# GpSimd's low-part subtractions of 1024 columns made in four instructions of 256 columns each

## The chip, the cores and the metric

The kernel runs on 1 core of one Trainium2 chip. The metric is the device time of one execution in microseconds (us): the median of 3 runs of the kernel before is 2904.75 us (2903.07 to 2905.82). Five engines work beside each other and meet only in semaphores: TensorE (PE; its weight loads are PEld), VectorE (DVE), ScalarE (ACT), GpSimd (POOL) and SyncE (SP, which only issues DMAs here).

## The reference, cut to what matters

A chain of two models over 512 tokens of width 1024: a first layer (compressed, selected and windowed attention, retention, a gated feed-forward network, FFN, with a causal depthwise convolution of width 3), and then a block of two layers (pooling, convolution and differential attention, a squared-ReLU network, a gated embedding). What matters for the change is the one shape in which nearly all of it is computed, a product of a weight with the activations:

```
proj = h @ w_in[layer]
u = causal_dwconv(h @ w_ffn_up[layer], ffn_conv_w[layer], ffn_conv_b[layer])
u_gate, u_val = jnp.split(u, 2, axis=-1)
x = x + (jax.nn.silu(u_gate) * u_val) @ w_ffn_down[layer]
```

Everything is in float32. The kernel makes a float32 product out of three fp32r products: each operand x is split into a high part, x rounded to fp32r, and a low part, x minus its high part, and w*a is w_hi*a_hi + w_hi*a_lo + w_lo*a_hi.

## The kernel before, in words

All weights are one stream, cut into units of 128 partitions by 1024 columns (`UNIT`); two units are a block, four a group. Each unit goes through four steps, on four engines:

1. SP loads a block into `raw` (two slots). Before it overwrites a slot it waits until the low parts of both units of the slot are made (`lo_done`, L294 to L295).
2. ACT copies a unit from `raw` to `w_hi`, which rounds it (`hi_part`, L385), once PE is done with the unit that had the place (`unit_done`): the part of unit u can be made when PE has finished unit u-4.
3. POOL subtracts, `w_lo = raw - w_hi` (`lo_part`, L316), once ACT's `hi_done` has risen, and raises `lo_done` by 1. It does this for 447 profiled units, in order.
4. PE waits for `lo_done` and for the PSUM bank (`evac`), and makes the unit's 24 matmuls with 512 moving columns, L635 to L637 (`unit` and `product`). DVE then reads the PSUM bank (L1059 and others) and does what the layer wants.

Each engine works in the order of its own program; POOL also does a small part of retention (L331 to L347, on 512 and 1024 columns) and seven additions of 512 columns in each layer of the second block (L361).

Around it DVE splits activations in the same way. In the FFN one tile of the hidden width takes two units of PE (gate, then value), and on DVE the sequence L1059, L1468, L1471, L1475 for the gate (into `tile_c`), the same four for the value (into `td`), and then L1484 (product), L1489 (`y_hi`) and L1491 (`y_lo`). L1059 reads one operand from PSUM; the others have all of theirs in SBUF. ACT's Silu of `tile_c` stands in ACT's order between the high parts of two pairs of units, so POOL gets its units in pairs there. The 22 tiles are made in three chunks of 8, 8 and 6; behind each chunk come 8 units of the down projection, which read all `y` tiles of the chunk and wait for each of them in turn.

In retention and in the layers' attention DVE makes the probabilities between two products of PE (L1255 to L1266; L1609 to L1614), and PE waits for the last of them.

At the end of a product that ends a layer part, DVE adds each unit to `h` (L1447), makes the next operand (L1077, L1080) and the sum of squares (L1086, L1090), and PE sums over partitions (L668).

Of the kernel before, what the change touches and what calls it, by code (L numbers as in the profile page):

```python
# [25 lines left out]
ALU = mybir.AluOpType  # L26
# [9 lines left out]
EPS = 1e-6  # L36
UNIT = 8 * P
BLOCK = 2 * UNIT


HEADS, KVG, DH = 8, 2, 64
# [21 lines left out]
U_CMP = NSA_UNITS  # L63
# [13 lines left out]
GROUPS = UNITS // 4  # L77
# [63 lines left out]
def build(nc, stream, xT, tab, decay, rope, par1, par2, pT, out):  # L141
    ctx = ExitStack()
    with ctx:
        def sb(name, shape, dt=F32):
            return ctx.enter_context(nc.sbuf_tensor(name, shape, dt))

        def sem(name):
            return ctx.enter_context(nc.semaphore(name))
# [10 lines left out]

        raw = sb("raw", [P, 2, BLOCK])  # L160
        w_hi = sb("w_hi", [P, 2, BLOCK], F32R)
        w_lo = sb("w_lo", [P, 2, BLOCK], F32R)

# [62 lines left out]
        lo_done = sem("unit_lo_done")  # L226
# [52 lines left out]
        def conv_unit_slot(j):  # L279
            return (j // 2) % 2, slice((j % 2) * UNIT, (j % 2 + 1) * UNIT)  # L280


        @block.sync
        def _(sp):

            sp.dma_start(par[:, 0:C1_FFN], par1[:, 0:C1_FFN]).then_inc(first_gain_landed, 16)
            for k in range(KD):
                sp.dma_start(h[:, k, :], xT[:, k, :]).then_inc(x_tile_landed[k], 16)
            sp.dma_start(raw[:, 0, UNIT:], stream[0, :, UNIT:]).then_inc(landed[0], 16)
            sp.dma_start(raw[:, 1], stream[1]).then_inc(landed[1], 16)  # L290
            with sp.Fori(1, GROUPS) as g:
                for s in range(2):

                    sp.wait_ge(lo_done, g * 4 - 2 + 2 * s)  # L294
                    sp.dma_start(raw[:, s], stream[g * 2 + s]).then_inc(landed[s], 16)  # L295

            for s in range(2):
                sp.wait_ge(lo_done, GROUPS * 4 - 2 + 2 * s)
                sp.dma_start(raw[:, s], stream[s]).then_inc(landed[s], 16)
            for s in range(2):  # L300
                sp.wait_ge(landed[s], 16 * (GROUPS + 1))

            for n in range(KD):
                sp.wait_ge(h_tile_ready, KD * LAYERS + n + 1)
                sp.dma_start(out[:, n, :], h[:, n, :]).then_inc(out_stored, 16)
            sp.wait_ge(out_stored, 16 * KD)


        @block.gpsimd
        def _(pool):  # L310
            def lo_part(u, j):

                s, cols = conv_unit_slot(j)

                pool.wait_ge(hi_done, u + 1)
                pool.tensor_tensor(w_lo[:, s, cols], raw[:, s, cols], w_hi[:, s, cols],  # L316
                                   ALU.subtract).then_inc(lo_done, 1)

            with pool.Fori(0, U_RET // 4) as g:
                for j in range(4):  # L320
                    lo_part(g * 4 + j, j)
            for j in range(3):
                lo_part(U_RET + j, j)

            with pool.Fori(0, RH) as t:
                for j in range(3, RET_UNITS + 3):
                    lo_part(t * RET_UNITS + U_RET + j, j % 4)

                pool.wait_ge(activated, t + 2)
                pool.wait_ge(squares_ready, t + 1)  # L330
                pool.tensor_tensor(rg[:, 0, :], rg[:, 0, :], rq, ALU.mult).then_inc(output_gated, 1)  # L331
                pool.tensor_tensor(rg[:, 1, :], rg[:, 1, :], rk, ALU.mult).then_inc(output_gated, 1)
                pool.wait_ge(output_gated, t * 2 + 2)

                pool.tensor_tensor(rg, rg, small[:, 24:26].unsqueeze(2).to_broadcast([P, 2, S]), ALU.mult)\
                    .then_inc(output_scaled, 1)
                pool.wait_ge(output_scaled, t * 3 + 1)

                pool.wait_ge(root_inverted, t + 1)
                for e in range(2):  # L340
                    pool.tensor_tensor(rg[:, e, :], rg[:, e, :], tile_c, ALU.mult)\
                        .then_inc(output_scaled, 1)
                pool.wait_ge(output_scaled, t * 3 + 3)
                hi, lo = (y[:, bass.ds(t * 2, 2), :] for y in (y_hi, y_lo))
                pool.tensor_copy(hi, rg).then_inc(output_rounded, 1)
                pool.wait_ge(output_rounded, t + 1)
                pool.tensor_tensor(lo, rg, hi, ALU.subtract).then_inc(y_tile_ready, 2)  # L347
            lo_part(U_YA + 3, 3)
            with pool.Fori(U_YA // 4 + 1, U_L // 4) as g:
                for j in range(4):  # L350
                    lo_part(g * 4 + j, j)
            with pool.Fori(0, LAYERS) as layer:
                ul = layer * L_UNITS + U_L
                for j in range(3):
                    lo_part(ul + j, j)

                for k in range(1, KD):
                    pool.wait_ge(x_square_ready, layer * KD + (KD + k + 1))
                    if k > 1:
                        pool.wait_ge(squares_added, layer * (KD - 2) + (k - 1))  # L360
                    ins = pool.tensor_tensor(ssum[:, :], m[:, 0, :] if k == 1 else ssum[:, :], m[:, k, :], ALU.add)  # L361
                    if k < KD - 1:
                        ins.then_inc(squares_added, 1)
                ins.then_inc(squares_ready, 1)
                lo_part(ul + 3, 3)
                with pool.Fori(1, L_UNITS // 4) as g:
                    for j in range(4):
                        lo_part(ul + g * 4 + j, j)
            for j in range(3):
                lo_part(GROUPS * 4 + j, j)  # L370
# [246 lines left out]
        def _(pe):  # L617
# [10 lines left out]
            def product(dst, w, rhs_hi, rhs_lo, nk, first=None, start=True, stop=True):  # L628

                s, c0 = w  # L630
                for k in range(nk):
                    if first is not None:
                        first(k)
                    cols = slice(c0 + k * P, c0 + (k + 1) * P)
                    pe.matmul(dst, w_hi[:, s, cols], rhs_hi(k), start=start and k == 0, stop=False)  # L635
                    pe.matmul(dst, w_hi[:, s, cols], rhs_lo(k), start=False, stop=False)  # L636
                    ins = pe.matmul(dst, w_lo[:, s, cols], rhs_hi(k), start=False,  # L637
                                    stop=stop and k == nk - 1)
                return ins

            def unit(u0, j, lag, dsts, rhs, nk, first=None, start=True, stop=True):


                s, cols = conv_unit_slot(j)
                pe.wait_ge(lo_done, u0 + (j + 1))
                pe.wait_ge(evac, u0 + (j + 5 - lag))
                hi, lo = rhs
                for o, dst in enumerate(dsts):
                    ins = product(dst, (s, cols.start + o * nk * P), hi, lo, nk,
                                  first if o == 0 else None, start, stop)  # L650
                ins.then_inc(unit_done, 1)
# [28 lines left out]
            def simple(u0, j, banks=2, first=None, nk=8):  # L680
                unit(u0, j, banks, [bank[j % banks][:, :]], a_op(), nk, first)
# [34 lines left out]
            def hidden_unit(kv, q):  # L716
                j = kv * 4 + q
                s, cols = conv_unit_slot(j)
                pe.wait_ge(lo_done, U_CMP + j + 1)
                if q == 0:  # L720

                    pe.wait_ge(evac, U_CMP + 3 + kv)
                dst = bank[kv][0:KVG * NCMP, 0:CMP_HIDDEN]
                for k in range(4):
                    w = slice(cols.start + k * CMP_HIDDEN, cols.start + (k + 1) * CMP_HIDDEN)
                    x_hi, x_lo = (x[kv][:, 4 * q + k].rearrange("p g c -> p (g c)") for x in (xc_hi, xc_lo))
                    pe.matmul(dst, x_hi, w_hi[:, s, w], start=q == 0 and k == 0, stop=False)
                    pe.matmul(dst, x_lo, w_hi[:, s, w], start=False, stop=False)
                    ins = pe.matmul(dst, x_hi, w_lo[:, s, w], start=False, stop=q == 3 and k == 3)
                ins.then_inc(unit_done, 1)  # L730
# [37 lines left out]
            with repeat(pe, RH, [(score, 8), (prb, 8), (ptp, 8), (ptr, 8), (pv, 8), (ofree, 1),  # L768
                                 (rin, 4), (rps, 9), (rfree, 8), (sums, 1), (sump, 1),
                                 (tin, 1)]) as t:  # L770
                u0 = t * RET_UNITS + U_RET
# [139 lines left out]
            with repeat(pe, LAYERS, [(a_rdy, 24), (y_rdy, 54), (sums, 15), (sump, 15), (tin, 4),  # L911
# [43 lines left out]
                for j in range(8):  # L955
                    if j == 7:
# [4 lines left out]
                         lambda k, j=j: square_sum((b_r0, b_r1)[(j - 1) % 2], ones2, (tile_b, tile_c)[(j - 1) % 2])  # L961
# [915 lines left out]
def _stream(x):  # L1877
# [54 lines left out]
    both = np.stack(units).reshape(UNITS // 2, 2, P, UNIT)  # L1932
    return np.ascontiguousarray(both.transpose(0, 2, 1, 3)).reshape(UNITS // 2, P, BLOCK)

# [57 lines left out]
```

## Time and profile before

| what | us |
| --- | --- |
| median of 3 runs | 2904.75 (2903.07 to 2905.82) |
| span of the profiled execution | 2901.3 |
| PE busy | 2688.2 (93%) |
| DVE busy | 1791.4 (62%) |
| POOL busy | 1162.9 (40%) |
| ACT busy | 798.3 (28%) |

The profile is of one execution: its span is from its first to its last instruction, and the runs' median is 3.4 us above it. Start and idle times in the views are in us from the start of the span. "Idle" is the time before an instruction in which its engine did nothing, and the name behind the arrow ended it. A DVE or POOL instruction counts as busy from the moment it is taken up, also while it stands still: a group whose minimum and maximum lie far apart on one shape has such standing time in it.

### The profile page before, as it was taken

The numbers are of one execution on the slowest core, as the hardware profiler recorded it, in microseconds if no ns is written. First come the engines' busy times: TensorE is split into PE (matmuls) and PEld (weight loads), VectorE is DVE, ScalarE is ACT, GpSimd is POOL, SyncE is SP. The second block draws the span as 40 slices with busy tenths as digits, with TensorE's granted clock in tenths as the row PEclk, the third lists the DMA queues.
The fourth block names the chain that finished last, engine by engine and source line by source line (L and its number), as shares of the span: only waits on it lengthen the run. The fifth ranks groups of instructions, "written<-read, shape, count | busy, mean of one in ns | idle before, by whom it ended". The sixth has DMA issues, their size and how long they took to land.

```text
span 2901.3 us, 33803 instructions
## 1 busy us (share of the span) xinstructions
PE 2688.2 (93%) x11835; PEld 2135.0 (74%) x11835; DVE 1791.4 (62%) x2170; ACT 798.3 (28%) x1178; POOL 1162.9 (40%) x493
## 2 busy tenths in 40 slices
PE   7898889999797978989999999999988999999998
PEld 5676666878586866667887788877766887788886
DVE  7566675368666586885238555473888136844484
ACT  2332333313221123433322121124333232211212
POOL 3523332543343444223444444445323444444444
PEclk9999999999898988999999999999999999999999
DMA  4301111322222221112222222222211222222222
GB/s 166 117 33 58 41 39 40 128 88 86 73 87 81 93 87 68 56 62 91 93 96 93 97 97 91 101 102 73 80 58 66 102 92 97 88 102 87 101 101 102
DMA packets 36822, 247.25 MB, mean 85 GB/s; under 512 B 4464, under 2 KB 4848, under 8 KB 7792
## 3 DMA queue, kind: packets, MB, share of 16 engines
q1 hardware_dynamic: 34704, 238.57, 23.2%
q10 hardware_dynamic: 2016, 7.35, 0.7%
q8 instruction: 61, 1.00, 0.1%
q14 instruction: 41, 0.34, 0.0%
HBM read 243.81 MB, written 2.10 MB: 85 GB/s over the span
## 4 chain that ended last, share of the span: by engine, by line
PE 62%; DVE 28%; issue 6%; ACT 1%; POOL 1%; DVEq 1%; ACTq 0%; POOLq 0%
PE bank L635 10%; PE bank L636 10%; PE bank L637 10%; PE both L635 9%; PE both L636 9%; PE both L637 9%; DVE td L1471 2%; DVE td L1475 1%; POOL w_lo L316 1%; DVE y_hi L1063 1%; DVE y_lo L1065 1%; ACT prob L466 1%; DVE small L1218 1%; DVE prob L1266 1%; PE bank L668 1%
## 5 line engine op out<-in xcount | busy, mean ns | idle before, releaser
L316 POOL TENSOR_TENSOR w_lo<-raw,w_hi 128x1024 fp32r<-128x1024 f32 x447 | 1102.0, 2469 | 1633.1 <-ACT w_hi L385 1627.1
L385 ACT ACTIVATE w_hi<-raw 128x1024 fp32r<-128x1024 f32 x446 | 468.4, 1056 | 1032.3 <-PE both L637 532.4
L635 PE MATMUL bank<-a_hi,w_hi 128*128 128x512 f32 x1369 | 564.5, 412 | 3.9 <-POOL w_lo L316 3.2
L637 PE MATMUL bank<-a_hi,w_lo 128*128 128x512 f32 x1369 | 538.8, 394 | 0.0
L636 PE MATMUL bank<-a_lo,w_hi 128*128 128x512 f32 x1369 | 538.2, 393 | 0.0
L635 PE MATMUL both<-a_hi,w_hi 128*128 128x512 f32 x864 | 348.8, 404 | 31.7 <-DVE a_lo L1526 18.9
L637 PE MATMUL both<-a_hi,w_lo 128*128 128x512 f32 x864 | 339.3, 393 | 0.0
L636 PE MATMUL both<-a_lo,w_hi 128*128 128x512 f32 x864 | 339.2, 393 | 0.0
L635 PEld LDWEIGHTS bank<-a_hi,w_hi 128*128 128x128 f32 x1369 | 261.1, 191 | 68.4 <-issue 12.4
L636 PEld LDWEIGHTS bank<-a_lo,w_hi 128*128 128x128 f32 x1369 | 261.1, 191 | 57.9 <-issue 7.3
L637 PEld LDWEIGHTS bank<-a_hi,w_lo 128*128 128x128 f32 x1369 | 259.9, 190 | 56.4
L635 PE MATMUL both<-y_hi,w_hi 128*128 128x512 f32 (+1 forms) x600 | 242.1, 403 | 62.0 <-DVE y_lo L1491 48.2
L636 PE MATMUL both<-y_lo,w_hi 128*128 128x512 f32 (+1 forms) x600 | 238.8, 398 | 0.0
L637 PE MATMUL both<-y_hi,w_lo 128*128 128x512 f32 (+1 forms) x600 | 238.1, 397 | 0.0
L635 PE MATMUL bank<-y_hi,w_hi 128*128 128x512 f32 (+1 forms) x600 | 235.9, 393 | 0.0
L636 PE MATMUL bank<-y_lo,w_hi 128*128 128x512 f32 (+1 forms) x600 | 234.2, 390 | 0.0
L637 PE MATMUL bank<-y_hi,w_lo 128*128 128x512 f32 (+1 forms) x600 | 234.0, 390 | 0.0
L635 PEld LDWEIGHTS both<-a_hi,w_hi 128*128 128x128 f32 x864 | 164.2, 190 | 74.1 <-DVE a_lo L1526 21.4
L636 PEld LDWEIGHTS both<-a_lo,w_hi 128*128 128x128 f32 x864 | 164.3, 190 | 37.9 <-issue 4.5
L637 PEld LDWEIGHTS both<-a_hi,w_lo 128*128 128x128 f32 x864 | 164.0, 190 | 34.7
L635 PEld LDWEIGHTS both<-y_hi,w_hi 128*128 128x128 f32 x600 | 115.5, 193 | 97.3 <-DVE y_lo L1491 51.6
L1063 DVE CAST y_hi<-ta 128x512 fp32r<-128x512 f32 x72 | 147.2, 2044 | 2.5
(272 smaller groups left out, 3270.1 us busy)
## 6 DMA issues: line engine op xcount, KB each, us to landing
raw<-stream SPq DMA_DIRECT2D x223, 1024.0 KB, 4.7
h<-xT SPq DMA_DIRECT2D x8, 256.0 KB, 6.3
h<-xT ACTq DMA_DIRECT2D x1, 2048.0 KB, 7.5
outT<-h SPq DMA_DIRECT2D x8, 256.0 KB, 2.4
h<-decay ACTq DMA_DIRECT2D x1, 1024.0 KB, 4.8
h<-rope ACTq DMA_DIRECT2D x1, 1024.0 KB, 7.0
prob<-pT ACTq DMA_DIRECT2D x2, 512.0 KB, 3.6
par<-par ACTq DMA_DIRECT2D x2, 408.0 KB, 3.1
```

The lines of the kernel that those rows point to most:

```text
L316: pool.tensor_tensor(w_lo[:, s, cols], raw[:, s, cols], w_hi[:, s, cols], ALU.subtract).then_inc(lo_done, 1)
L385: act.activation(w_hi[:, s, cols], raw[:, s, cols], ACT.Copy).then_inc(hi_done, 1)
L466: ins = act.activation(dst, src, ACT.Exp, bias=small[:, b:b + 1], scale=last_scale, accum_out=small[:, b + 4:b + 5])
L635: pe.matmul(dst, w_hi[:, s, cols], rhs_hi(k), start=start and k == 0, stop=False)
L636: pe.matmul(dst, w_hi[:, s, cols], rhs_lo(k), start=False, stop=False)
L637: ins = pe.matmul(dst, w_lo[:, s, cols], rhs_hi(k), start=False, stop=stop and k == nk - 1)
L668: pe.matmul((b_r1 if dst is None else dst)[:, :], ones if w is None else w, ssum[:, :] if src is None else src, start=True, stop=True)\
L1063: V.tensor_copy(y_hi[:, at, :], src).then_inc(vector_step, steps.up())
L1065: V.tensor_tensor(y_lo[:, at, :], src, y_hi[:, at, :], ALU.subtract)\
L1218: V.tensor_reduce(small[:, 8 + cmp:10 + cmp], scores[:, :, 0:n], AX.X, ALU.max)\
L1266: V.tensor_scalar(prob[:, 1, 0:n], prob[:, 1, 0:n], small[:, 14:15], gate[2], ALU.mult, ALU.mult).then_inc(probs_ready, prb.up())
L1471: V.scalar_tensor_tensor(out=dst, in0=buf[:, 15:15 + S], scalar=cw[1], in1=dst, op0=ALU.mult, op1=ALU.add)\
```

## The change

Each subtraction of 1024 columns in `lo_part` becomes four of 256 columns, one behind the other, each of which raises `lo_done` by 1; so `lo_done` counts quarters, and all waits for it (SP's before a load, PE's before a unit and before a unit of the compression) are multiplied by four. No engine waits for a single quarter: PE and SP go on when the fourth is done.

```
+LO_PARTS = 4
@@ sync
-                    sp.wait_ge(lo_done, g * 4 - 2 + 2 * s)
+                    sp.wait_ge(lo_done, g * (4 * LO_PARTS) + (2 * s - 2) * LO_PARTS)
-                sp.wait_ge(lo_done, GROUPS * 4 - 2 + 2 * s)
+                sp.wait_ge(lo_done, (GROUPS * 4 - 2 + 2 * s) * LO_PARTS)
@@ gpsimd, lo_part
-                pool.tensor_tensor(w_lo[:, s, cols], raw[:, s, cols], w_hi[:, s, cols],
-                                   ALU.subtract).then_inc(lo_done, 1)
+                for q in range(LO_PARTS):
+                    part = slice(cols.start + q * UNIT // LO_PARTS, cols.start + (q + 1) * UNIT // LO_PARTS)
+                    pool.tensor_tensor(w_lo[:, s, part], raw[:, s, part], w_hi[:, s, part],
+                                       ALU.subtract).then_inc(lo_done, 1)
@@ tensor, unit
-                pe.wait_ge(lo_done, u0 + (j + 1))
+                pe.wait_ge(lo_done, u0 * LO_PARTS + (j + 1) * LO_PARTS)
@@ tensor, hidden_unit
-                pe.wait_ge(lo_done, U_CMP + j + 1)
+                pe.wait_ge(lo_done, (U_CMP + j + 1) * LO_PARTS)
```

POOL's program in the loop that covers the rest of the first layer (the one over groups at L349 of the kernel before), one group of four units, before:

```order
L316 TENSOR_TENSOR w_lo<-raw,w_hi 128x1024 [waits unit_hi_done]
L315 REGISTER_ALU
L316 TENSOR_TENSOR w_lo<-raw,w_hi 128x1024 [waits unit_hi_done]
L315 REGISTER_ALU
L316 TENSOR_TENSOR w_lo<-raw,w_hi 128x1024 [waits unit_hi_done]
```

The same place of POOL after the change; the lines have moved down by three:

```order
L319 TENSOR_TENSOR w_lo<-raw,w_hi 128x256 [waits unit_hi_done]
L319 TENSOR_TENSOR w_lo<-raw,w_hi 128x256 x3
L316 REGISTER_ALU
L319 TENSOR_TENSOR w_lo<-raw,w_hi 128x256 [waits unit_hi_done]
L319 TENSOR_TENSOR w_lo<-raw,w_hi 128x256 x3
```

The order of the units is as before; the first quarter carries the wait for ACT, and the other three follow it without one. PE's program at the head of a loop over FFN tiles, the first unit of an iteration, before:

```order
L131 UNCONDITIONAL_BRANCH
L131 ISA
L635 MATMUL both<-a_hi,w_hi 128x512 [waits unit_evacuated,unit_lo_done]
L636 MATMUL both<-a_lo,w_hi 128x512
L637 MATMUL both<-a_hi,w_lo 128x512
```

And after the change:

```order
L132 UNCONDITIONAL_BRANCH
L132 ISA
L649 REGISTER_ALU [waits unit_lo_done]
L638 MATMUL both<-a_hi,w_hi 128x512 [waits unit_evacuated]
L639 MATMUL both<-a_lo,w_hi 128x512
L640 MATMUL both<-a_hi,w_lo 128x512
```

In the loops PE has one more register instruction ahead of most units, which works out the multiplied value and takes over the wait for the low part; no matmul has moved. In the retention loop such an instruction stood there before as well, and a second is added to it.

## Rows read from the trace of the kernel before

**Rows 1.** The page, part 1 (its first figures), and part 5, POOL's largest group.

```profile
PE 2688.2 (93%) x11835; PEld 2135.0 (74%) x11835; DVE 1791.4 (62%) x2170; ACT 798.3 (28%) x1178; POOL 1162.9 (40%) x493
...
L316 POOL TENSOR_TENSOR w_lo<-raw,w_hi 128x1024 fp32r<-128x1024 f32 x447 | 1102.0, 2469 | 1633.1 <-ACT w_hi L385 1627.1
```

**Rows 2.** Waits of PE, whole span: us in total, times, longest us.

```profile
PE both L635 <- DVE y_lo L1491: 48.2, 6, 9.5
PE both L808 <- DVE prob L1266: 34.4, 13, 8.2
...
PE bank L941 <- DVE prob L1614: 21.2, 16, 2.7
...
PE bank L668 <- DVE ssum L1090: 14.3, 3, 5.6
PE both L635 <- DVE y_lo L1065: 11.0, 9, 2.2
...
PE bank L635 <- POOL w_lo L316: 3.2, 2, 2.4
```

**Rows 3.** Forms of L1471, L1059, L1526: ns min/median/max, first and last start.

```profile
L1471 DVE SCALAR_TENSOR_TENSOR td<-tb,par,td x22: 751/2926/2948, 676.8 to 1047.8; 128x512 f32<-128x512 f32 x22
...
L1059 DVE TENSOR_TENSOR ta<-bank,rstd x57: 690/692/694, 70.8 to 2890.6; 128x512 f32<-128x512 f32 x57
...
L1526 DVE SCALAR_TENSOR_TENSOR a_lo<-h,mix_gain,a_hi x16: 745/747/1781, 1100.4 to 2005.4; 128x512 fp32r<-128x512 f32 x16
```

**Rows 4.** Timeline of DVE, two FFN tiles: start us, us, instruction.

```profile
703.32 2.94 DVE L1471 SCALAR_TENSOR_TENSOR td<-tb,par,td 128x512 f32<-128x512 f32 x1
706.41 2.65 DVE L1475 SCALAR_TENSOR_TENSOR td<-tb,par,td 128x512 f32<-128x512 f32 x1
...
718.15 2.66 DVE L1484 TENSOR_TENSOR td<-td,tile_c 128x512 f32<-128x512 f32 x1
720.96 2.40 DVE L1489 CAST y_hi<-td 128x512 f32 x1
...
729.79 2.92 DVE L1471 SCALAR_TENSOR_TENSOR td<-tb,par,td 128x512 f32<-128x512 f32 x1
```

**Rows 5.** Timeline of POOL, the first of the same two tiles.

```profile
703.32 5.19 POOL L316 TENSOR_TENSOR w_lo<-raw,w_hi 128x1024 fp32r<-128x1024 f32 x2 [6.74 <-ACT w_hi L385]
```

**Rows 6.** Timelines: POOL's 512-column products in retention; DVE beside POOL's additions L361.

```profile
202.23 1.26 POOL L331 TENSOR_TENSOR work<-work,h 128x512 f32<-128x512 f32 x1 [4.36 <-DVE ssum L1389]
203.45 1.28 POOL L332 TENSOR_TENSOR work<-work,h 128x512 f32<-128x512 f32 x1
...
1101.77 8.19 DVE L1526 SCALAR_TENSOR_TENSOR a_lo<-h,mix_gain,a_hi 128x512 fp32r<-128x512 f32 x6
```

**Rows 7.** Stretches: us, busy us (instructions) of each engine, PEclk, DMA share, GB/s.

```profile
670.00:1090.00 420.00, 363.07 (x1541) 294.70 (x1539) 288.35 (x281) 89.77 (x97) 168.13 (x68) 0.93 0.24 85
...
1580.00:1900.00 320.00, 318.11 (x1397) 261.49 (x1396) 177.28 (x167) 63.11 (x60) 144.45 (x59) 1.00 0.27 95
```

**Rows 8.** Timeline of PE where the first chunk's down projection begins.

```profile
764.15 0.80 PE L635 MATMUL both<-y_hi,w_hi 128*128 128x512 f32 x1 [5.97 <-DVE y_lo L1491]
...
775.25 0.80 PE L635 MATMUL both<-y_hi,w_hi 128*128 128x512 f32 x1 [9.45 <-DVE y_lo L1491]
```

**Rows 9.** Timelines of POOL and DVE, a retention head's second group.

```profile
228.51 7.05 POOL L316 TENSOR_TENSOR w_lo<-raw,w_hi 128x1024 fp32r<-128x1024 f32 x3
...
231.00 2.31 DVE L1264 TENSOR_SCALAR work<-work,small 128x31 f32<-128x31 f32 x1
```

**Rows 10.** Timelines of DVE and PE, end of a layer's squared-ReLU network.

```profile
1931.79 2.26 DVE L1077 TENSOR_SCALAR a_hi<-h,par 128x512 fp32r<-128x512 f32 x1
1934.08 2.90 DVE L1080 SCALAR_TENSOR_TENSOR a_lo<-h,par,a_hi 128x512 fp32r<-128x512 f32 x1
...
1938.49 2.07 PE L668 MATMUL bank<-ssum,cst 128*128 128x512 f32 x2 [5.56 <-DVE ssum L1090]
```

**Rows 11.** Timeline of POOL in the compression.

```profile
107.40 7.15 POOL L316 TENSOR_TENSOR w_lo<-raw,w_hi 128x1024 fp32r<-128x1024 f32 x3 [0.42 <-ACT w_hi L385]
```

**Rows 12.** Forms of L646 and L645 on PE's queue: ns min/median/max, first and last start.

```profile
L646 PEldq ALU_OP  x128: 32/32/42, 115.0 to 2859.2; - x128
...
L645 PEldq ALU_OP  x222: 32/32/36, 122.0 to 2886.4; - x111
```

## The prediction, made before the changed kernel was run

> **What bounds the kernel now.** I read the page's shares first: PE is busy for 2688.2 of 2901.3 us [rows 1], so at most 213 us can be won without taking a matmul away, and the question is who holds PE up in those. The waits of PE answer it: nearly all of the long ones end with a DVE instruction (48.2 us on `y_lo` of the FFN, 34.4 us on retention's probabilities, 21.2, 14.3 and 11.0 us on three others), and next to nothing with POOL (3.2 us) [rows 2]. POOL itself waits 1627.1 us for ACT [rows 1]. So a faster or slower POOL matters little for its own sake, and DVE's speed at a few places matters.
>
> Then I asked of those DVE instructions whether they take as long as they must. They don't: L1471 on `td` is one shape, with a minimum of 751 ns and a median of 2926 [rows 3]. The timelines show what it stands for. At 703.32 POOL and L1471 begin together; L1471 takes 2.94 us instead of 0.75, and ends at 706.26, while POOL's pair of units runs to 708.51. L1475 begins at 706.41 and takes 2.65 instead of 0.75 [rows 4, 5]. So a DVE instruction on SBUF data stands still while one POOL unit runs, gets in between two units, and the next one stands for the second unit. L1484 and L1489 show the same at 718.15 and 720.96 [rows 4]. L1059, with one operand in PSUM, never does: 690 to 694 ns over 57 instances [rows 3].
>
> The Trainium skill's SBUF page (SBUF — State Buffer, section "Who interferes with whom") says the same of this pair: a DVE instruction with two SBUF inputs, or in a two-port mode, and a GpSimd instruction that reads SBUF exclude each other, and whoever comes first keeps the port for its whole instruction. By that rule the length of the POOL instruction is what a DVE instruction pays, and the rows above agree (2.19 and 1.90 us).
>
> **What a 256-column piece costs DVE.** I need the time by which the piece outlasts the DVE instruction ahead of it, since POOL gets its turn there. For 1024 columns: L1475 stands 2.65 - 0.75 = 1.90 us and had begun 0.15 us after the end of L1471, so 2.05 us [rows 4]. For 512 columns: L1526 stands 1.781 - 0.745 = 1.04 us beside L361 [rows 3]; in the stretch of six, two free and four held ones add up to 8.61 us in 8.19, so each begins 0.08 us before the one ahead has ended, which gives 0.96 us [rows 3, 6]. A line through both has 2.13 ns a column and gives 0.41 us for 256. A DVE instruction behind the usual gap of 0.15 us then stands some 0.27 us, one that begins early 0.49 us, and one that starts together with the first piece 2.19 - 768 x 2.13 ns = 0.55 us. Bounds: nothing, where the piece runs beside L1059 or while DVE is idle; 1.04 us, if a short instruction held DVE as long as the 512-column one. I take the line, which has two measured points, and keep both ends.
>
> **The FFN, step by step.** Two tiles take 26.47 us (703.32 to 729.79), 13.24 a tile, of which 2.19 + 1.90 + 1.97 + 1.97 over two tiles is standing time [rows 4]: 4.0 a tile, 9.2 without. PE needs two units of 24 matmuls: 318.11 / 1397 = 0.228 us a matmul at full clock [rows 7], 10.9 us. So DVE falls behind by 2.3 us a tile, 18 to 19 over a chunk of eight, and PE waits for it when the down projection wants the last `y` tiles: 5.97 and 9.45 us in the first chunk [rows 8], 48.2 in six waits for the three chunks [rows 2]. After the change a tile has eight pieces. Starting with L1484: 0.5, then 0.27 and 0.29; L1059 (0.69 us and its gaps, off the port) lets two pieces by almost free, 0.1; the last three cost 0.27, 0.27 and nothing beside the other L1059. Sum 1.7. Starting with L1471 it is 2.0. A tile is then 10.9 to 11.2 us, DVE holds PE's pace within 0.3 us, and what is left is the latency of the last tile: some 5 us of DVE work behind the last value unit with 1 to 2 us of pieces, against 7/8 of a unit (4.8 us) that PE can do meanwhile, plus a small backlog. I put what PE still waits at 3 us a chunk: 48 - 9 = **-39 us**. PE also works at the lower clock there (granted 0.93 [rows 7]): 1541 matmuls at 363.07/1541 - 0.228 = 0.008 us are 12 us, of which I give back 5: **-5**.
>
> **Retention.** Three units of POOL in a row (7.05 us) meet L1261, L1264 and L1266, which stand 2.1 us each (L1264: 2.31 us for an instruction on 31 columns) [rows 9]; PE waits up to 8.2 us for L1266, 34.4 in 13 waits [rows 2]. With pieces each stands at most 0.49 us: 6.2 becomes 1.5, -4.7, three times; in some five other waits one unit holds L1266, 1.3 us each. 14 + 6 = 20, of which I take **-18**, since DVE's remaining pieces fall on its next instructions.
>
> **Other ends.** L1077 and L1080 stand 1.77 and 2.15 us behind the last unit of a layer part, and DVE was already behind from the units ahead; PE waits 5.56 us [rows 10], 14.3 in all [rows 2]. I take -10. Of the 11.0 and 21.2 us on L1065 and L1614 [rows 2] I take -6 and -5, about 1 us where a held instruction stands last, and -2 at the start of the program. Together **-23**.
>
> **What it costs.** POOL: 512 columns take 1.26 us and follow each other after 1.22 [rows 6], 1024 take 7.15 / 3 = 2.38 [rows 11]. By the line a piece takes 0.64 to 0.70 and four 2.6 to 2.8: +0.2 to +0.4 a unit. POOL's 1627.1 us of waiting for ACT [rows 1] cover that nearly everywhere. They don't in the compression, where PE takes a unit as fast as POOL makes it: 8 units x 0.3 = **+2.5**. Beside DVE a pair of units stretches from 5.19 us to eight turns of about 1.0, and POOL has 6.74 us free ahead of the pair now [rows 5]; that is just enough at 11 us a tile. SP's loads start by as much later; a slot has the time of two units. Stretched units also meet DVE instructions that were free before; for all of that **+5**.
>
> The GPSIMD Engine Reference of the Trainium skill ("Performance versus the Vector engine", section 3.1) speaks against the change: it measures 4497 ns for a two-input instruction of 2048 elements. Beside the 2.38 us for 1024 here, an estimate from that page is 0.26 us fixed for each instruction, +0.8 us a unit and +6 instead of +2.5 in the compression; no run of before has 256 columns.
>
> PE: one more register instruction ahead of each unit in the loops. PE has such ones now, of 32 ns (128 that also wait for `lo_done`, 222 that don't) [rows 12], and through the loop of 1580 to 1900 with them its matmuls follow at 0.228 us without idle time [rows 7]: nothing. If they were exposed it would be 447 x 0.032 = +14 us, which I keep for the upper end.
>
> **Sum.** -39 - 5 - 18 - 23 + 2.5 + 5 = -77.5 on a span of 2901.3, so 2824 for the span, and with the 3.4 us by which the median lies above it, 2827 us.
>
> **The rivals.**
> - *The standing time is only spread.* POOL needs the port just as long; if each of the four pieces meets a DVE instruction that has begun early, it is 4 x 0.49 = 1.96 us, what one unit costs now. For it: DVE is dense there, busy 288 of 420 us [rows 7]. Against it: the gaps of 0.15 us and L1059 in each tile. A tile is then 13.24 - 4.0 + 2.6 = 11.8 us, the backlog 7 us a chunk; the FFN gives 22 instead of 44, the rest about half of 41, the costs stay: -35, about 2870 us.
> - *DVE does not get in between pieces.* No engine waits between them, and the GPSIMD page (section 2.1) says that a GpSimd core begins its next instruction as soon as its own share is done. If the port then stayed with POOL over all four, DVE would stand as now and only the costs were left: 2904.75 + 2.5, about 2907. Against it stands L1471, which ended 2.2 us before POOL's pair [rows 4, 5], though POOL's second unit was ready as well.
> - *Slower: a piece holds DVE as long as 512 columns do.* At 1.04 us a piece the six pieces that meet the port in a tile cost 6.2 instead of 4.0, +2.2 x 22 tiles = +48 in the FFN, a third of that elsewhere: about 2970 us. It decides from 0.67 us a piece, where six make 4.0. Against it: 512 and 1024 columns lie on a line through nearly zero. The exposed register instruction has the same sign and adds to its chance.
>
> **How the numbers follow.** Chances: forecast 0.67, spread 0.20, not between 0.05, slower 0.08. Faster by over 0.2% (6 us, about what a measurement of this kernel can tell from no change) are the first two, 0.87; within 0.2% 0.05; slower 0.08. The forecast's own range is 2800 to 2858: all of PE's waits on held instructions gone, with the clock, or half of the terms outside the FFN missing and one more us a tile. The range that is to hold it 8 times in 10 reaches into the spread case: 2797 to 2882.
>
> **What would show it.** L1471 on `td` at some 1.0 to 1.3 us instead of 2.93; two FFN tiles in about 22 us; the six waits on `y_lo` L1491 near 9 us in all instead of 48.2; L808's wait on L1266 near 15 instead of 34.4; a 256-column piece of 0.6 to 0.75 us where it runs alone; POOL busy above 1250 us, and PE's waits for the low part still below 10. DVE busy should fall by at least 50 us (22 tiles x 2.2). The forecast is wrong if L1471 still takes over 2 us, if PE's units in the loops lie further apart than 5.5 us, or if waits on POOL appear in the FFN.

## The result, and the profile after

| | before | after |
| --- | --- | --- |
| median, us | 2905.28 (2903.07 to 2905.86, 4 runs) | 2792.52 (2791.57 to 2793.81, 4 runs) |
| span of the profiled execution, us | 2901.3 | 2790.2 |
| mean granted clock | 0.970 | 0.984 |

The ratio is 0.9614, with a 95% interval of 0.9600 to 0.9627: 112.8 us less where 77.5 were forecast. The time lies 4.5 us below the range. Lines of the kernel below the change stand 3 further down in the program after (L1471 is L1474, L635 is L638).

First the page's busy times and POOL's largest group, which answer to [rows 1]:

```profile
PE 2665.6 (96%) x11835; PEld 2128.5 (76%) x11835; DVE 1553.8 (56%) x2170; ACT 800.2 (29%) x1178; POOL 1542.7 (55%) x1834
...
L319 POOL TENSOR_TENSOR w_lo<-raw,w_hi 128x256 fp32r<-128x256 f32 x1788 | 1481.4, 859 | 1153.1 <-ACT w_hi L388 1147.3
```

POOL is busy 380 us longer and DVE 238 us shorter, with DVE's 2170 instructions the same. POOL took more time, and PE paid for little of it (the compression, below). PE too is busy 22.6 us less, for the same 11,835 matmuls.

PE's waits, which answer to [rows 2] (us in total, times, longest us):

```profile
PE both L638 <- DVE y_lo L1494: 14.1, 3, 6.3
PE bank L944 <- DVE prob L1617: 13.2, 15, 1.9
PE both L811 <- DVE prob L1269: 10.0, 3, 3.3
PE both L638 <- POOL w_lo L319: 9.7, 1, 9.7
...
PE both L638 <- DVE y_lo L1068: 6.6, 5, 2.2
PE bank L671 <- DVE ssum L1093: 6.5, 3, 2.3
PE bank L730 <- POOL w_lo L319: 4.1, 4, 1.2
```

The first two of [rows 2], 48.2 and 34.4 us, are 14.1 and 10.0 now. The single wait of 9.7 us for POOL is at the start of the program, where the profile before has one of the same 9.7 us for DVE (`a_lo` L1080). Its length stayed, but not its cause: before, POOL's first unit ended at 8.43 us and DVE, held behind it, had its first `a_lo` at 9.50; after, DVE is done at 8.12 and POOL, stretched over four pieces, at 9.58. So nothing was won there.

The forms that answer to [rows 3] (ns min/median/max, first and last start):

```profile
L1474 DVE SCALAR_TENSOR_TENSOR td<-tb,par,td x22: 750/1278/1287, 647.8 to 976.8; 128x512 f32<-128x512 f32 x22
```

```profile
L319 POOL TENSOR_TENSOR w_lo<-raw,w_hi x1788: 712/741/1692, 6.0 to 2784.3; 128x256 fp32r<-128x256 f32 x199
```

L1474 on `td` has gone from a median of 2926 ns to 1278, out of a minimum of 750: 0.53 us of standing time in place of 2.18. A piece of 256 columns takes 0.71 us at its fastest and 0.74 in the median.

Now two FFN tiles on DVE and POOL's work beside the second of them, which answer to [rows 4, 5] (start us, us, instruction):

```profile
658.75 0.75 DVE L1474 SCALAR_TENSOR_TENSOR td<-tb,par,td 128x512 f32<-128x512 f32 x1
...
669.82 1.28 DVE L1474 SCALAR_TENSOR_TENSOR td<-tb,par,td 128x512 f32<-128x512 f32 x1
671.24 1.00 DVE L1478 SCALAR_TENSOR_TENSOR td<-tb,par,td 128x512 f32<-128x512 f32 x1
672.37 1.02 DVE L1487 TENSOR_TENSOR td<-td,tile_c 128x512 f32<-128x512 f32 x1
...
680.79 0.75 DVE L1474 SCALAR_TENSOR_TENSOR td<-tb,par,td 128x512 f32<-128x512 f32 x1
```

```profile
669.81 7.83 POOL L319 TENSOR_TENSOR w_lo<-raw,w_hi 128x256 fp32r<-128x256 f32 x8 [2.25 <-ACT w_hi L388]
```

POOL's eight pieces and L1474 begin together at 669.8. L1474 stands for one piece (0.53 us), L1478 for the rest of one (0.25), and so on: DVE gets in between pieces, and POOL's pair stretches from 8 x 0.74 = 5.9 to 7.83 us. From L1474 to L1474 two tiles take 22.04 us instead of 26.47.

Where the rest of the time went is read from stretches of both kernels that begin at the same matmul of PE: start to retention, retention, the units up to the FFN, the FFN, and all behind it. Before (us, busy us of each engine, PEclk, DMA share, GB/s):

```profile
0.00:171.00 171.00, 141.33 (x676) 108.79 (x677) 112.08 (x180) 54.88 (x96) 68.23 (x33) 0.97 0.36 128
171.00:546.00 375.00, 339.75 (x1609) 251.27 (x1608) 228.09 (x420) 122.95 (x277) 124.94 (x63) 0.96 0.15 53
546.00:646.00 100.00, 97.19 (x426) 79.24 (x425) 55.80 (x55) 22.25 (x24) 44.77 (x18) 1.00 0.27 95
646.00:1067.00 421.00, 367.19 (x1562) 298.76 (x1561) 287.51 (x286) 92.48 (x99) 162.87 (x67) 0.93 0.23 80
1067.00:2901.30 1834.30, 1742.72 (x7569) 1396.90 (x7567) 1107.88 (x1231) 505.69 (x682) 762.12 (x315) 0.98 0.25 88
```

and after, with a stretch of full units below, which answers to the second of [rows 7]:

```profile
0.00:168.65 168.65, 141.74 (x676) 110.02 (x677) 102.03 (x180) 55.13 (x96) 96.10 (x117) 0.96 0.37 129
168.65:518.10 349.45, 335.12 (x1609) 249.30 (x1608) 199.37 (x420) 123.05 (x278) 146.88 (x168) 0.99 0.16 57
518.10:618.55 100.45, 98.44 (x425) 80.31 (x424) 46.74 (x57) 22.23 (x24) 59.91 (x71) 0.98 0.26 92
618.55:994.60 376.05, 362.00 (x1561) 297.83 (x1560) 234.50 (x284) 94.07 (x99) 234.78 (x263) 0.97 0.26 90
994.60:2790.20 1795.60, 1728.36 (x7568) 1391.02 (x7567) 971.13 (x1230) 505.76 (x682) 1005.00 (x1218) 0.99 0.26 90
1499.00:1813.00 314.00, 314.00 (x1385) 259.74 (x1384) 136.76 (x164) 63.13 (x60) 190.88 (x234) 1.00 0.28 97
```

A stretch less PE's busy time is PE's idle time. With it each stage's change splits in two:

| stage | idle, before to after | change of idle | forecast | change of PE busy |
| --- | --- | --- | --- | --- |
| start, compression | 29.7 to 26.9 | -2.8 | +0.5 | +0.4 |
| retention | 35.3 to 14.3 | -20.9 | -18 | -4.6 |
| up to the FFN | 2.8 to 2.0 | -0.8 | | +1.3 |
| FFN | 53.8 to 14.1 | -39.8 | -39 | -5.2 |
| behind it | 91.6 to 67.2 | -24.3 | -21 + 5 | -14.4 |
| sum | 213.1 to 124.5 | **-88.6** | **-72.5** | **-22.5** |

The forecast's one term for PE's busy time was -5, in the FFN.

### The profile page after: what moved, and what is told of

The parts are those of the page before. It is cut to its first block, busy times and chain, and to the rows that moved or that the text cites. A ratio compares the mean times of both kernels' runs of the same rounds, so it can differ in the third digit from the quotient of the medians.

```text
span 2790.2 us, 35262 instructions
## 1 busy us (share of the span) xinstructions
PE 2665.6 (96%) x11835; PEld 2128.5 (76%) x11835; DVE 1553.8 (56%) x2170; ACT 800.2 (29%) x1178; POOL 1542.7 (55%) x1834
## 4 chain that ended last, share of the span: by engine, by line
PE 75%; DVE 16%; issue 4%; POOL 2%; ACT 1%; DVEq 1%; ACTq 0%; POOLq 0%
PE bank L638 13%; PE bank L639 12%; PE bank L640 12%; PE both L638 11%; PE both L639 11%; PE both L640 10%; POOL w_lo L319 2%; DVE small L1221 1%; PE bank L671 1%; ACT prob L469 1%; PE both L804 1%; DVE prob L1617 1%; DVE td L1474 1%; PE both L805 1%; PE bank L792 1%
## 5 line engine op out<-in xcount | busy, mean ns | idle before, releaser
L319 POOL TENSOR_TENSOR w_lo<-raw,w_hi 128x256 fp32r<-128x256 f32 x1788 | 1481.4, 859 | 1153.1 <-ACT w_hi L388 1147.3
L638 PE MATMUL bank<-a_hi,w_hi 128*128 128x512 f32 x1369 | 560.3, 409 | 0.0
L638 PE MATMUL both<-a_hi,w_hi 128*128 128x512 f32 x864 | 349.1, 404 | 30.6 <-DVE a_lo L1529 19.0
L638 PEld LDWEIGHTS bank<-a_hi,w_hi 128*128 128x128 f32 x1369 | 259.0, 189 | 62.0 <-issue 10.8
L638 PE MATMUL both<-y_hi,w_hi 128*128 128x512 f32 (+1 forms) x600 | 239.1, 399 | 22.3 <-DVE y_lo L1494 14.1
L638 PE MATMUL bank<-y_hi,w_hi 128*128 128x512 f32 (+1 forms) x600 | 236.0, 393 | 0.0
L638 PEld LDWEIGHTS both<-a_hi,w_hi 128*128 128x128 f32 x864 | 164.4, 190 | 71.8 <-DVE a_lo L1529 21.4
L638 PEld LDWEIGHTS both<-y_hi,w_hi 128*128 128x128 f32 x600 | 115.0, 192 | 51.0 <-DVE y_lo L1494 15.3
L1450 DVE TENSOR_TENSOR h<-bank,h 128x512 f32<-128x512 f32 x56 | 38.7, 692 | 172.9 <-PE bank L640 172.9
```

Of the source, the lines that this page charges most:

```text
L319: pool.tensor_tensor(w_lo[:, s, part], raw[:, s, part], w_hi[:, s, part], ALU.subtract).then_inc(lo_done, 1)
L1450: leave(u0, j, V.tensor_tensor(h[:, n, :], bank4(j), h[:, n, :], ALU.add))
```

## The experiments

Each ran beside the kernel before. Its median was 2904.54 us beside the bookkeeping, two and eight pieces, and the FFN alone; 2904.53 beside the last two; and 2905.48 beside the others.

**The bookkeeping alone.** All waits and counts as in the change, but one instruction:

```
-                for q in range(LO_PARTS):
-                    ... four subtractions of 256 columns, then_inc(lo_done, 1)
+                pool.tensor_tensor(w_lo[:, s, cols], raw[:, s, cols], w_hi[:, s, cols],
+                                   ALU.subtract).then_inc(lo_done, LO_PARTS)
```

> One instruction of 1024 columns again, which raises the count of low parts by 4; every wait is multiplied by 4, as in the changed kernel, so PE has the additional register instructions. Theory (the length of the instruction that holds the port is what DVE pays): nothing is won, 2905 us within 6, L1474 on td stays at 2.93 us. Rival (part of the gain is from the waits, or the register instructions cost something that the pieces hide): 10 us or more away from 2905.

Measured: 2900.57 us (2899.38 to 2902.70), ratio 0.9986 (0.9976 to 0.9996). The form of the FFN's instruction:

```profile
L1472 DVE SCALAR_TENSOR_TENSOR td<-tb,par,td x22: 750/752/2985, 679.6 to 1047.1; 128x512 f32<-128x512 f32 x22
```

The gain is the pieces', not the bookkeeping's, and the register instruction on PE's queue costs nothing. The form is a warning: its median fell to 752 ns with next to nothing won, because POOL's units now meet the instructions behind it (L1476 takes 2.65 us at 707.0 and L1485 2.69 at 709.8). The median of one line doesn't measure standing time; DVE's busy time does (1791.4 before, 1780.4 here, 1553.8 after). The 4 us that are won lie mostly in the FFN, whose stretch, cut at the same matmuls, takes 417.5 us in place of 421.0; why is open.

**Other sizes.** `LO_PARTS` 2, 8 and 16, so 512, 128 and 64 columns:

```
-LO_PARTS = 4
+LO_PARTS = 2        (and 8, 16)
```

> Two pieces of 512 columns. Theory: a held DVE instruction stands 0.8 to 1.1 us instead of 1.9 to 2.2 (and 0.25 to 0.5 in the changed kernel), two pieces of four still pass beside instructions off the port; L1474 on td near 1.8 us; an FFN tile near 11.7 us; time about 2840. Rival (only the number of places counts at which DVE may get in, the total standing time is the same): within 20 us of 2905.

> Eight pieces of 128 columns. Theory: standing time of a held instruction falls to 0 to 0.25 us, but a piece costs POOL 0.13 us beside its columns (4 x 0.71 against 2.35 us in the changed kernel), so a unit takes about 3.5 us alone and the compression gets 5 us slower; what is left to win on PE's waits is small: 2775 to 2800 us. Rival (POOL becomes the bound, PE waits for low parts): over 2830 us with waits of PE on the low part in the FFN and retention.

> Sixteen pieces of 64 columns. A line through the pieces that ran alone (1.26 us for 512, 0.72 for 256, 0.45 for 128) gives 0.3 us for 64, 4.8 us a unit, where PE takes a unit every 5.4 us. Theory: DVE stands no less than with eight (nothing is left), and POOL becomes the bound in the compression and near it elsewhere: slower than eight, 2785 to 2830 us. Rival (shorter pieces go on winning because DVE's instructions get in faster): under 2769 us.

| pieces | columns | median us | ratio (interval) | piece, ns min/median | POOL busy | DVE busy | PE busy | PE idle | clock |
| --- | --- | --- | --- | --- | --- | --- | --- | --- | --- |
| 1 | 1024 | 2904.54 | | (2380) | 1162.9 | 1791.4 | 2688.2 | 213.1 | 0.970 |
| 2 | 512 | 2852.21 | 0.9821 (0.9805 to 0.9838) | 1256/1295 | 1305.0 | 1729.6 | 2671.0 | 177.3 | 0.977 |
| 4 | 256 | 2792.52 | 0.9614 (0.9600 to 0.9627) | 712/741 | 1542.7 | 1553.8 | 2665.6 | 124.6 | 0.984 |
| 8 | 128 | 2768.83 | 0.9528 (0.9512 to 0.9544) | 443/460 | 1862.9 | 1429.4 | 2654.2 | 115.4 | 0.990 |
| 16 | 64 | 2819.18 | 0.9713 (0.9696 to 0.9729) | 307/321 | 2440.3 | 1453.5 | 2665.9 | 142.3 | 0.986 |

Idle is the span less PE busy. The FFN's instruction with two and with eight pieces:

```profile
L1474 DVE SCALAR_TENSOR_TENSOR td<-tb,par,td x22: 750/1834/1842, 660.7 to 1016.8; 128x512 f32<-128x512 f32 x22
```

```profile
L1474 DVE SCALAR_TENSOR_TENSOR td<-tb,par,td x22: 750/751/754, 644.5 to 959.7; 128x512 f32<-128x512 f32 x22
```

Its standing time is 2.18, 1.08, 0.53 and 0.00 us for 1024, 512, 256 and 128 columns. The two-piece kernel came out 12 us above what was expected, the one with eight pieces 6 us below its range (2775 to 2800), and the one with sixteen inside its own. The two-piece kernel missed although its instruction stands as long as the line said: PE's wait for `y_lo` is still 40.9 us there, since DVE is still slower than PE in the FFN. With eight pieces two instructions go against the rule. The timelines of POOL and DVE around the first:

```profile
1031.29 16.71 POOL L319 TENSOR_TENSOR w_lo<-raw,w_hi 128x128 fp32r<-128x128 f32 x40 [6.58 <-ACT w_hi L388]
```

```profile
1041.95 6.60 DVE L1572 TENSOR_TENSOR tb<-ta 128x512 f32<-128x512 f32 x1
```

L1572 (0.69 us where it is free; both of its operands are in SBUF) begins inside POOL's run of 40 pieces and ends at 1048.55, half a microsecond behind the run's end at 1048.00: it was shut out over some 15 pieces. The second rival of the prediction is thus real in two places (the other is at 1922.87), and false in nearly all others. With sixteen pieces POOL itself becomes late. PE's waits there:

```profile
PE both L638 <- POOL w_lo L319: 27.7, 17, 16.2
...
PE bank L730 <- POOL w_lo L319: 14.1, 6, 2.8
PE bank L638 <- POOL w_lo L319: 8.6, 9, 1.4
```

That is 50.4 us of waits for the low part. The same three were 6.5 us before (3.2 of them in [rows 2]). Sixteen pieces of 0.32 us are 5.1 us a unit, and more with DVE beside them, where PE takes a unit in 24 x 0.227 = 5.45: POOL has no time to spare.

**One stage alone.** Four pieces only in the FFN's 68 units, or only in retention's:

```
+            with pool.Fori(U_FFN // 4, U_L // 4) as g:
+                for j in range(4):
+                    lo_part(g * 4 + j, j, LO_PARTS)       # all others: one piece
```

> Four pieces only for the 68 units of the FFN of the first layer; all other units in one instruction. Theory: the FFN's share of the gain and nothing else. By the two traces the stretch from 652 to 1097 us of before became 43 us shorter: 2862 us within 5. Rival (the gain of one stage comes with what another stage does, for instance POOL that arrives late): more than 10 us away from it.

> Four pieces only for the 32 units of the retention loop; all others in one instruction. The prediction gave this stage 18 us; the two traces show 26 us less from 171 to 546 us of before. Theory (the stage is worth PE's waits on the probabilities that vanish, 24 us, and the matmuls that no longer run at the lower clock behind those waits): 2879 us within 3, with PE busy for some 6 us less than in the kernel before. Rival (the term was right, and the rest of the 26 us comes from the other stages' pieces): 2887 us.

Measured: FFN alone 2859.77 us (2856.99 to 2860.31), ratio 0.9843 (0.9827 to 0.9860); retention alone 2877.38 (2872.54 to 2878.80), 0.9901 (0.9885 to 0.9918). Two waits of PE in the first, and the FFN's in the second:

```profile
PE both L814 <- DVE prob L1272: 35.3, 13, 8.5
...
PE both L641 <- DVE y_lo L1497: 14.0, 3, 6.3
```

```profile
PE both L638 <- DVE y_lo L1494: 46.1, 6, 9.2
```

Each stage's waits fall where its pieces are. The small fall of the FFN's wait in the second (48.2 to 46.1) is in the kernel with the bookkeeping alone too, also 46.1. The two gains, 44.8 and 28.1 us, make 72.9; the whole change wins 112.8, so 40 come from other stages (some 4 more, as the bookkeeping's 4 us are in both). In the retention kernel idle time is 213.1 - 188.6 = 24.5 us less, but PE busy only 2.6 less (2685.6), where 6 were expected: a miss.

**The low parts without a read.** The low parts are left out; POOL fills `w_lo` with zeros instead, one instruction a unit:

```
-                ... the four subtractions
+                pool.memset(w_lo[:, s, cols].bitcast(F32), 0.0).then_inc(lo_done, LO_PARTS)
```

> Leaves out the low parts of the weights: POOL sets w_lo to zero in one instruction of 1024 columns, which writes but reads nothing, with the same counts and waits. It asks which side of the port is in dispute. Theory, with the rule of the Trainium skill's page SBUF — State Buffer, Who interferes with whom (two SBUF inputs on DVE exclude a GpSimd instruction that reads, not one that only writes; a two-port mode excludes both): L1474 on td at 0.75 us throughout, the cast and the tensor_scalar still held now and then by up to the length of the memset; time 2760 to 2800. Rival (the two engines exclude each other whatever they do): L1474 held by the memset's length.

Measured: 2743.19 us (2738.30 to 2743.48), ratio 0.9436 (0.9421 to 0.9452). The forms of POOL's instruction, and of two of DVE's:

```profile
L317 POOL MEMSET w_lo<- x447: 944/955/1248, 6.1 to 2733.2; 128x1024 f32 x149
```

```profile
L1471 DVE SCALAR_TENSOR_TENSOR td<-tb,par,td x22: 750/752/756, 644.9 to 960.0; 128x512 f32<-128x512 f32 x22
```

```profile
L1468 DVE TENSOR_SCALAR tile_c<-ta,par x22: 545/910/1347, 640.8 to 954.1; 128x512 f32<-128x512 f32 x22
```

The time is 17 us below the expected range (2760 to 2800): POOL's instruction is shorter as well, so the time alone says nothing of the port, but the two forms do. L1471, with two SBUF inputs, is never held by POOL's write of 0.95 us, though 18 of the 22 begin while one runs, by a count over the trace; L1468, with one, is, by up to 0.8 us. The Trainium skill ("SBUF — State Buffer", section "Who interferes with whom") says just this: two SBUF inputs contend with a GpSimd instruction that reads SBUF and not with one that only writes, while `tensor_scalar` can run in a mode that takes both ports. The trace agrees on both. The counts and waits are those of the change, and all operands of L1471 and of POOL's instruction are in SBUF. So the shared port, not semaphores or PSUM, is the place where L1471 stood.

**Eight pieces without their costs.** One instruction a unit for the first unit, the compression's eight and the three behind them, where PE waits for POOL, and L361's additions, all but the last, in four instructions of 128 columns:

```
+            for j in range(4):
+                lo_part(j, j, 1 if j == 0 else LO_PARTS)          # LO_PARTS = 8
...
+            with pool.Fori(U_CMP // 4, U_RET // 4) as g:          # compression: one piece
+                for j in range(4):
+                    lo_part(g * 4 + j, j, 1)
```

> Eight pieces for most units; one instruction for the first unit, for the eight of the compression and the three behind it, where DVE has little to do; POOL's additions of 512 columns in the layers in four of 128 (but the last). Theory: e3_eight_parts less some 5 us of the compression and 1 to 2 at the start, less 1 us a layer at the additions: 2760 us within 4. Rival (the compression is held by the loads, not by POOL): 2768.

Measured: 2767.04 us (2764.71 to 2770.08), ratio 0.9521 (0.9505 to 0.9537); eight pieces throughout have 2768.83. The forecast of 2760 missed. The rival's number (2768) came true, but not its reason, that the loads hold the compression: by the starts of the same DVE instructions in both traces everything behind the compression is 5.1 us earlier than with eight pieces throughout. Of that 0.5 us is lost again in the first layer's head and 3.0 in the second's. Against the kernel with four pieces the two heads are 8.8 and 10.0 us longer, and one instruction stands in each:

```profile
L1581 DVE TENSOR_TENSOR tb<-ta x8: 691/692/6720, 1037.7 to 1970.1; 128x512 f32<-128x512 f32 x8
```

**Eight pieces, four in the layers' heads.** As the kernel just above, but the first twelve units of each layer in pieces of 256, once with the additions whole and once with them in four:

```
+                for j in range(3):
+                    lo_part(ul + j, j, 4)
...
+                lo_part(ul + 3, 3, 4)
+                with pool.Fori(1, 3) as g:
+                    for j in range(4):
+                        lo_part(ul + g * 4 + j, j, 4)
```

> Eight pieces of 128 columns as in the run before this one (unit 0, the compression's units and three behind them in one instruction each), but four pieces of 256 in the first twelve units of each layer of the second block, where DVE stood 6.03 and 5.57 us beside a run of 128-column pieces and the heads came out 5.8 and 10.3 us late; POOL's seven additions of 512 columns per layer are whole. The theory (DVE is not let in between short pieces that run without a pause) expects 2767 - 5.8 - 10.3 + 1 to 2 for the whole additions = 2752, within 5, and no DVE instruction of the heads standing above 2 us. The rival (the heads are held by something else, such as the units' loads or PE's waits on sums) expects no change, 2767, and late heads as before.

> As the run beside it, with the additions of 512 columns (POOL, seven per layer, all but the last of each) in four instructions of 128 columns. If short pieces that wait for nothing shut DVE out, this is 0 to 5 us slower than its neighbour, since additions come in rows of four too; if only the length of one instruction counts, it is 1 to 2 us faster. Theory: within 2 us of its neighbour, about 2752; rival: 2767 for both.

Measured: 2751.16 us (2748.32 to 2753.59), ratio 0.9471 (0.9458 to 0.9484), and 2753.42 (2752.17 to 2755.40), 0.9478 (0.9465 to 0.9491). The first is the best kernel here that makes the low parts, 153 us below before. PE is busy 2649.5 us and DVE 1422.8 in its profile. The form of the instruction that had stood, and POOL beside it:

```profile
L1580 DVE TENSOR_TENSOR tb<-ta x8: 691/692/1162, 1036.7 to 1950.3; 128x512 f32<-128x512 f32 x8
```

```profile
1026.10 11.20 POOL L319 TENSOR_TENSOR w_lo<-raw,w_hi 128x256 fp32r<-128x256 f32 x16 [7.19 <-ACT w_hi L396]
```

The expectation was met, and most of the late heads came from those two instructions: they had stood 6.03 and 5.57 us, 11.6 of the 16 us won. The second kernel is 2.3 us slower than its neighbour, where at most 2 either way were expected; in its profile the second layer's head is 5.3 us longer by the starts of the same DVE instructions, so cutting the additions won nothing, and why is open. It isn't shown that pieces of 256 would have let DVE in there. POOL makes a unit of four pieces in 2.8 us and one of eight in 3.34 (16.71 / 5), so it is further on, and its run ends at 1037.30, 0.6 us behind the start of L1580 (1036.7). What was tested is that DVE isn't shut out when little of the run is left.

## Why the prediction was wrong, and where it was right

**The direction and the mechanism held.** DVE stood for the rest of whatever POOL instruction had the port, and with short ones it gets in between. The rival without that (2907 us) is refuted by L1474's 1278 ns, and the slower one by the same row: 0.53 us a piece, below the 0.67 from which it would decide. The rival of spread standing time had a tile at 11.8 us; it takes 11.0, and DVE's busy time fell by 238 us.

**The FFN term was right.** Forecast -39 in waits, measured -39.8 in idle time; forecast -5 by the clock, measured -5.2 in PE's busy time (3.4 of it at the lower clock, as below). A tile of 11.0 us was forecast at 10.9 to 11.2. What PE still waits for `y_lo` is 14.1 us, not 9, with 6.3 us the longest, in the first chunk, in place of the two waits of [rows 8].

The step of 13.24 us a tile was sound because both the standing time and PE's pace were in rows.

**The steps that failed are the term for PE's busy time and the sizes outside the FFN.** The prediction gave back 5 us of clock, in the FFN alone, since that was the one stretch whose 0.93 it had read [rows 7], and put all other stages at nothing without a reason. PE's busy time fell by 22.5 us, 17.3 of them elsewhere, above all 4.6 in retention and 14.4 behind the FFN. That is one half of the miss; the other, 16.1 us, are waits (further below). Neither alone takes the time out of the range (2827 - 17.5 = 2809.5, 2827 - 16.1 = 2810.9).

Stretches of 25 us around a retention wait and around the wait of [rows 10] show how it comes about. Before:

```profile
320.00:345.00 25.00, 16.83 (x73) 11.96 (x72) 17.80 (x24) 5.01 (x15) 12.93 (x7) 0.80 0.23 84
1925.00:1950.00 25.00, 19.25 (x73) 14.46 (x72) 19.34 (x18) 6.04 (x8) 11.22 (x5) 0.86 0.23 80
```

After:

```profile
305.00:330.00 25.00, 21.68 (x102) 15.22 (x101) 20.49 (x36) 6.82 (x18) 17.29 (x18) 1.00 0.23 84
1838.00:1863.00 25.00, 21.99 (x88) 17.03 (x87) 17.63 (x19) 8.43 (x9) 19.16 (x24) 0.93 0.36 126
```

Each of the waits of 5 to 8 us left PE some microseconds at 1.2 instead of 2.4 GHz behind it. In such a stretch the lower clock holds for twice the missing share: 0.20 x 2 x 25 = 10 us and 7 us before, nothing and 3.5 us after. About half of this lay in the wait itself and cost nothing: PE was busy for 4.5 and 4.2 us of it before. The retention wait had been up to 8.2 us and is 3.3 at most, the other went from 5.56 to 2.07. Two of the three waits of 3.3 us are still followed by 3.4 us at the lower clock; the one shown is the third. The timeline of PE behind that second wait shows the price:

```profile
1848.23 1.24 PE L671 MATMUL bank<-ssum,cst 128*128 128x512 f32 x2 [2.07 <-DVE ssum L1093]
...
1850.12 0.63 PE L640 MATMUL bank<-y_hi,w_lo 128*128 128x512 f32 x1
1850.55 0.63 PE L638 MATMUL bank<-y_hi,w_hi 128*128 128x512 f32 x1
...
1853.54 0.39 PE L638 MATMUL both<-y_hi,w_hi 128*128 128x512 f32 x1
1853.77 0.40 PE L639 MATMUL both<-y_lo,w_hi 128*128 128x512 f32 x1
```

Matmuls follow each other after 0.43 us at 1850 and after 0.23 at 1853.5. So a wait can have a second price. How much of the 22.5 us is that? By a sum over the clock records of both traces, the lower clock stood for 173.5 us before, of which PE was busy in 91.8, and for 91.1 us after, with 62.2 busy. At the lower clock the matmuls take about twice as long (0.43 and 0.23 us above), so PE's busy time held 45.9 us for the clock and holds 31.1: -14.8, by stage +2.2, -3.2, +1.7, -3.4 and -12.1. The other 7.7 us lie in matmuls at full clock, most of them within eight matmuls behind a wait of before.

Which waits the clock came back from isn't shown. In the kernel with four pieces in retention alone, that stage's idle time is 14.3 us, just as with the whole change, but PE works there at the lower clock for 15.0 us, against 13.2 before and 6.8 with the whole change: the same waits gone, and nothing given back. How much would come back wasn't in any row; it could be bounded from above by the 45.9 us.

**Retention and the other ends were right in kind, small in size.** Retention: -18 forecast, -20.9 in idle time; over the whole span the wait itself fell by 24.4 us, to 10.0 where some 15 was written down. An L1269 wait is now 3.3 us at most, of 8.2. POOL and DVE there, which answer to [rows 9]:

```profile
225.08 9.83 POOL L319 TENSOR_TENSOR w_lo<-raw,w_hi 128x256 fp32r<-128x256 f32 x12
```

```profile
225.09 0.93 DVE L1264 TENSOR_SCALAR prob<-prob,small 128x384 f32<-128x384 f32 x1
225.94 0.70 DVE L1267 TENSOR_SCALAR work<-work,small 128x31 f32<-128x31 f32 x1
226.55 0.94 DVE L1269 TENSOR_SCALAR prob<-prob,small 128x384 f32<-128x384 f32 x1
```

Each of the three stands 0.45 to 0.47 us (their minima on these shapes are 0.47, 0.23 and 0.48), as the "at most 0.49" of the prediction had it; the discount from 20 to 18 was not needed. Behind the FFN L671's wait fell by 7.8 us (10 forecast), L638's for L1068 by 4.4 (6), and L944's for L1617 by 8.0 (5): -20.2 in sum where 21 were forecast, and the idle time fell by 24.3. The 2 us at the start of the program weren't won, as shown above, but the first stage as a whole lost 2.8 us of idle time where 0.5 more was forecast; 1.0 of that is one wait on L1062 (9.9 to 8.9 us), the rest is open.

**The costs were half there.** The 5 us for late low parts and extra hits didn't appear: -24.3 behind the FFN is more than the gains alone. PE's waits for the low part are 13.8 us after, above the 10 that the prediction named as a sign, but 9.7 of that is the wait at the start. The cost in the compression did appear: sixteen pieces without a pause give 11.34 / 16 = 0.71 us each, 2.84 a unit against 2.38 [rows 11], +0.45 where 0.2 to 0.4 was forecast; by the starts of the same DVE instructions in both traces the stage takes 2.0 us more (2.5 forecast). POOL there:

```profile
103.30 11.34 POOL L319 TENSOR_TENSOR w_lo<-raw,w_hi 128x256 fp32r<-128x256 f32 x16 [0.44 <-ACT w_hi L388]
```

PE's register instruction was rightly put at nothing: in the stretch of full units PE is busy 314.00 of 314 us at 0.227 us a matmul.

**The sum of the misses.** PE's busy time 17.5 us and waits 16.1 us are the 33.6 us of profiled time between -77.5 and -111.1. The waits are 8.3 us behind the FFN (5 of them the cost that didn't come), 3.3 in the first stage, 2.9 in retention, and 0.8 each in the FFN and ahead of it. The lower end of the prediction's own range, 2800, is close to 2904.75 - 48 - 20 - 23 - 12 = 2802: all of the FFN's waits, the 20 of retention, the 23 of the other ends and the 12 us of clock of the FFN. It had nothing for PE's busy time elsewhere, and so the one error sat in the sum and in the bound.

## What to carry to other kernels

Where one engine holds a shared port for the length of its instruction, cut the long instructions of the engine that has time to spare; the price is a fixed cost a piece, so the best size lies where that engine is just not late: here 128 columns, 256 in the layers' heads, and whole units where TensorE waits for them. When a change takes waits away from TensorE, price its busy time too, over the whole program and not only in the stage looked at. What the clock can give back is at most half of the time that TensorE works at the lower clock (here 45.9 us, of which 14.8 came back). And measure standing time by the busy time of the waiting engine, since a single line's median can fall with nothing won.

## What the hardware showed beside that

- A DVE instruction was shut out over some fifteen 128-column pieces in a row (6.60 and 6.62 us instead of 0.69, twice with eight pieces, and 6.72 and 6.26 in the kernel with whole units in the compression), each time the same one, L1572 behind L1062 (L1581 behind L1071 in the other kernel). In the eight-piece kernel some 900 DVE instructions began with at least three pieces of a run to come, by a count over the trace, and none but these two stood over 0.4 us beside them. What sets these apart is open.
- A GpSimd subtraction takes 0.31, 0.44, 0.71, 1.26 and 2.38 us for 64, 128, 256, 512 and 1024 columns at its fastest (the last as a mean of a run): 2.1 ns a column and some 0.17 us that each instruction adds. The GPSIMD Engine Reference of the Trainium skill (section 3.1), weighed in the prediction, gave 0.26 by an estimate; the pieces cost less.
- POOL's own 1024-column instructions of retention still hold DVE: L1261 stands 1.7 us in three heads (1.95 us instead of 0.25), with pieces of 256, 128 and 64 columns alike.
